# A triangular inverse on VectorE: each final column taken off the columns to its right

## What is computed

```python
lmat = jnp.where(strict, jnp.einsum('bhncd,bhnmd->bhncm', k_beta, k) * decay, 0.0)
tmat = lax.linalg.triangular_solve(eye + lmat, jnp.broadcast_to(eye, lmat.shape),
                                   left_side=True, lower=True, unit_diagonal=True)
u = jnp.einsum('bhncm,bhnmd->bhncd', tmat, v_beta)
w = jnp.einsum('bhncm,bhnmd->bhncd', tmat, k_beta * jnp.exp(gc)[..., None])
```

## Time and profile before

| | us |
|---|---|
| median of 3 runs | 1786.27 |
| lowest and highest | 1786.02, 1787.35 |
| the profiled execution | 1793.27 |
| its span, first to last instruction | 1791.5 |

### The profile page before, as it was taken

How to read it: one execution, slowest core, us unless ns; L and a number is a source line. 1 busy time by engine, 2 the same in 40 slices (tenths; PEclk the granted TensorE clock), 3 DMA queues, 4 the chain that set the end, 5 groups by cost and what they waited for, 6 DMA issues and landing times.

```text
span 1791.5 us, 27755 instructions
## 1 busy us (share of the span) xinstructions
PE 1599.2 (89%) x11576; PEld 1390.4 (78%) x11576; DVE 1022.5 (57%) x1683; ACT 735.2 (41%) x1135; POOL 54.5 (3%) x68
## 2 busy tenths in 40 slices
PE   4998866899989997877899999987999999999987
PEld 2786656888878775655677777766989999999987
DVE  3755799677663655789655554555334343434543
ACT  5555532435345414532224243454543232324454
POOL 0000000000000030000000000000000000000000
PEclk9999978989999988988899999999999999999999
DMA  6254323223232332312221223324323232323222
GB/s 183 79 141 119 88 63 89 75 65 82 61 108 81 80 76 80 96 55 65 66 69 45 60 63 89 99 74 130 100 77 95 83 94 83 95 83 95 87 71 83
DMA packets 281026, 153.37 MB, mean 86 GB/s; under 512 B 36997, under 2 KB 272637, under 8 KB 280894
## 3 DMA queue, kind: packets, MB, share of 16 engines
q1 hardware_dynamic: 279879, 150.32, 29.8%
q10 hardware_dynamic: 1022, 1.28, 0.3%
HBM read 135.03 MB, written 16.97 MB: 85 GB/s over the span
## 4 chain that ended last, share of the span: by engine, by line
PE 68%; DVE 16%; ACT 7%; issue 4%; DMA 4%; ACTq 0%; SPq 0%; POOL 0%; DVEq 0%; POOLq 0%
PE ps L1295 56%; DVE prod L1874 3%; DVE of L1955 3%; PE ps L1429 2%; DVE Xp L1875 2%; DVE w_lo L1628 2%; PE ps L1458 2%; PE ps L1452 1%; DMA w_raw<-in_w_up 1%; DVE tk L1850 1%; ACT L920 1%; PE ps L1278 1%; PE ps L1419 1%; DMA qt<-qkv_dram 1%; ACT w_hi L916 1%
## 5 line engine op out<-in xcount | busy, mean ns | idle before, releaser
L916 ACT ACTIVATE w_hi<-w_raw 128x1024 fp32r<-128x1024 f32 (+3 forms) x258 | 232.7, 902 | 321.1 <-DMA w_raw<-in_w_down 177.9
L1295 PE MATMUL ps<-hh_hi,w_hi 128*128 128x256 f32 (+1 forms) x960 | 323.3, 337 | 30.0 <-DVE w_lo L1628 24.3
L1295 PE MATMUL ps<-hh_lo,w_hi 128*128 128x256 f32 (+1 forms) x960 | 316.7, 330 | 0.0
L1295 PE MATMUL ps<-hh_hi,w_lo 128*128 128x256 f32 (+1 forms) x960 | 315.5, 329 | 0.0
L1628 DVE TENSOR_TENSOR w_lo<-w_raw,w_hi 128x1024 fp32r<-128x1024 f32 (+3 forms) x258 | 266.8, 1034 | 56.5 <-ACT w_hi L916 55.2
L1295 PE MATMUL ps<-u_hi,w_hi 128*128 128x512 f32 (+2 forms) x768 | 260.1, 339 | 24.5 <-DVE w_lo L1628 13.3
L1295 PE MATMUL ps<-u_lo,w_hi 128*128 128x512 f32 (+2 forms) x768 | 253.0, 329 | 0.0
L1295 PE MATMUL ps<-u_hi,w_lo 128*128 128x512 f32 (+2 forms) x768 | 252.0, 328 | 0.0
L1295 PE MATMUL ps<-hm_hi,w_hi 128*128 128x512 f32 (+5 forms) x600 | 212.0, 353 | 28.2 <-DVE w_lo L1628 10.0
L1295 PEld LDWEIGHTS ps<-hh_hi,w_hi 128*128 128x128 f32 x960 | 185.8, 194 | 54.6 <-DVE w_lo L1628 33.9
L1295 PE MATMUL ps<-hm_lo,w_hi 128*128 128x512 f32 (+5 forms) x600 | 201.1, 335 | 0.0
(11 more groups left out here) (274 smaller groups left out, 2169.9 us busy)
## 6 DMA issues: line engine op xcount, KB each, us to landing
w_raw<-in_w_up SPq DMA_DIRECT2D x64, 512.0 KB, 4.1
w_raw<-in_w_in SPq DMA_DIRECT2D x48, 512.0 KB, 4.2
w_raw<-in_w_down SPq DMA_DIRECT2D x64, 256.0 KB, 2.8
w_raw<-in_w_down SPq DMA_DIRECT2D x32, 512.0 KB, 3.7
w_raw<-in_w_out SPq DMA_DIRECT2D x16, 512.0 KB, 3.8
w_raw<-in_w_ple_gate SPq DMA_DIRECT2D x16, 512.0 KB, 3.8
qt<-qkv_dram SPq DMA_DIRECT2D x8, 768.0 KB, 5.5
xin<-in_x_prompt SPq DMA_DIRECT2D x8, 512.0 KB, 6.5
```

Of the source, the lines that this page charges most:

```text
L916: nc.scalar.activation(w_hi[job.slot][:, 0:job.kts, 0:job.m], w_raw[job.slot][:, 0:job.kts, 0:job.m], ACT.Copy).then_inc(w_hid, 1)
L1295: last = nc.tensor.matmul(dst, wt[job.slot][:, k, 0:m], x[:, k, lo:hi], start=(i == 0 and n == 0), stop=(end and n == 2), skip_group_check ...
```

## The change

```diff
--- before.py
+++ after.py
@@ -179,11 +179,11 @@
         h = adv(h)
         put(h, "lp", s)
         put(h, "inv0", s)
-        total, c = sum(x * x + 60 for x in range(1, C)), 1
+        cost = [(x + 1) * (C - 1 - x) + 120 for x in range(C - 1)]
+        c = 0
         for i in range(n):
-            lo, spent = c, sum(x * x + 60 for x in range(1, c))
-            while c < C and (spent < total * (i + 1) / n or i == n - 1):
-                spent += c * c + 60
+            lo = c
+            while c < C - 1 and (sum(cost[:c]) < sum(cost) * (i + 1) / n or i == n - 1):
                 c += 1
             h = adv(h)
             put(h, "inv", s, lo, c)
@@ -1870,10 +1870,11 @@
             def inverse_columns(s, first, end):
                 dve.wait_ge(lt_ld, 16 * (s + 1))
                 for c in range(first, end):
-                    pr = prod[:, 0:c * c].rearrange("p (m j) -> p m j", j=c)
-                    step(nc.vector.tensor_tensor(pr, Xm[:, 0:c, 0:c], bc(Lm[:, 0:c, c], 1, c), ALU.mult))
-                    ins = nc.vector.tensor_reduce(Xm[:, 0:c, c], pr, AX, ALU.add, negate=True)
-                    if c < C - 1:
+                    n = C - 1 - c
+                    pr = prod[:, 0:(c + 1) * n].rearrange("p (m j) -> p m j", j=n)
+                    step(nc.vector.tensor_tensor(pr, bc(Xm[:, 0:c + 1, c], 2, n), bc(Lm[:, c, c + 1:C], 1, c + 1), ALU.mult))
+                    ins = nc.vector.tensor_tensor(Xm[:, 0:c + 1, c + 1:C], Xm[:, 0:c + 1, c + 1:C], pr, ALU.subtract)
+                    if c < C - 2:
                         step(ins)
                     else:
                         ins.then_inc(inv, 1)
```

## The result

The changed kernel takes 1748.33 us, the median of 4 runs (1746.65 to 1750.71), against 1786.14 us for the kernel before in the same session (4 runs, 1785.58 to 1787.35). The ratio is 0.9778 with a 95% interval of 0.9757 to 0.9799: faster, by 37.8 us. The forecast was 1751 us, a saving of 34.9 us, in a range of 1745 to 1760.

What follows compares the result with a forecast made beforehand. DVE was taken to bound both inverse stretches. 1793.27 - 36.4 (DVE) + 1.5 (later engines) = 1758.4 us for the profiled execution; the 34.9 us saving off the median 1786.27 gave 1751 us, range 1745 to 1760.

Steps and rivals of the forecast that it cites:

- The bound: In the stretches of the two inverses, A (69.03 us) and B (69.62 us), DVE has no slack and PE has a lot.
- The old cost: Old column steps: 1.83 ns per product number, 1.05 per sum number, 41.4 us of DVE per inverse.
- The new cost: New column steps: 0.19 us fixed each, 1.04 ns per number, 23.2 us of DVE per inverse.
- rival of the strided column: New product still pays for reading `Xm` with 128 bytes between rows: 8.6 us of gain lost, 1760 us; chance 0.08.
- A price per row: Rival: product and subtraction pay per row jump in `Xm`; break-even 18 ns, at 40 ns 1829 us; slower, chance 0.02.
- What is late next: Check of what becomes late in A and B once DVE needs 50.8 and 51.4 us; 1.5 us allowed in all.
- last `up` jobs of B: Jobs of 24 matmuls where PE or its weights' transfer would be later than DVE by a few tenths of a us.
- PE's wait for ACT in A: One wait of 9.5 us until ACT empties a PSUM bank; claimed to end with a DVE step and move with it.
- rival of PE at the lower clock: PE becomes the bound in A and B: at most 24 us of gain lost, 1759 us (1755 to 1763); chance 0.17.
- wait for the inverses behind B: PE waits 2.21 us for the inverse read back; up to 1.5 us may go, nothing counted.
- The 7 us of the profiled execution: Profiled execution lies 7 us above the runs' median; taken as a difference between executions, so the saving comes off the median.
- more than the DVE time: Rival: PE keeps the upper clock behind either stretch, and the wait behind B shrinks: 3 to 6 us more, 1746 us; chance 0.06.

Runs made afterwards that it cites:

- e1: Kernel before, its old product reading adjacent numbers of a row of Lp instead of a column 128 bytes apart: 1773.76 us, ratio 0.9919.
- e2: Changed kernel, its product reading Lp down a column, 128 bytes apart, instead of along a row: 1761.79 us, ratio 0.9856.
- e5: Changed kernel with only the last of the 31 columns of each inverse computed: 1718.49 us, ratio 0.961.
- e3: Kernel before with the new form for the inverse of half 1 (stretch B) alone: 1771.88 us, ratio 0.9909.
- e4: Kernel before with the new form for the inverse of half 0 (stretch A) alone: 1768.4 us, ratio 0.9887.
- e0: Changed kernel run once more with no edit: 1748.18 us, ratio 0.9784.
- e6: Changed kernel with the columns of half 1 dealt out to 30 stages instead of 12: 1731.57 us, ratio 0.9702; again 1736.2 us, ratio 0.9713.

## Why the prediction came out right

**The bound.** The reading that DVE has no slack in A and B, and that a microsecond less on it is a microsecond less in the end, held. 36.4 us were taken off DVE's queue and the two windows became 138.65 - 102.31 = 36.3 us shorter.

**The old cost** is measured by e1 in the other way: without the stride the product has the price of the sum, 1.16 us for 961 numbers. The 1.83 and 1.05 ns were right.

**The new cost.** 1.04 ns for both steps and 0.19 us fixed gave 0.42 us for the middle column and 23.2 us per inverse; both were measured. L1824 and L1857 were the right neighbours. The rival of the strided column is excluded by the row of 0.42 us, and e2 shows what it would have looked like, 0.62 us and 9 us of time. The prediction gave it 8.6.

**A price per row** is nearly nothing. Products of A in ns: the first column has its 31 numbers in 1 row and the last in 31 rows; the second has its 60 numbers in 2 rows and the last but one in 30:

```profile
L1875 DVE TENSOR_TENSOR prod<-Xp,Lp x1: 186/186/186, 228.3 to 228.3; 128x31 f32<-128x31 f32 x1
L1875 DVE TENSOR_TENSOR prod<-Xp,Lp x1: 209/209/209, 278.9 to 278.9; 128x31 f32<-128x31 f32 x1
...
L1875 DVE TENSOR_TENSOR prod<-Xp,Lp x1: 221/221/221, 228.7 to 228.7; 128x60 f32<-128x60 f32 x1
L1875 DVE TENSOR_TENSOR prod<-Xp,Lp x1: 222/222/222, 278.4 to 278.4; 128x60 f32<-128x60 f32 x1
```

30 more rows cost 23 ns in the last column (20 in its subtraction; 19 and 27 in B), about 0.8 ns each, where 18 ns were needed for no gain. 28 more rows cost 1 ns where a row has two numbers (3 in the subtraction). The start of a row as such is free. The Trainium skill, SBUF — State Buffer, in its note on "cachelines", has every crossing to a new 16-byte line pay the extra cost, and the last column crosses with every number in `Xm`. By this case's price of a crossing, 0.79 ns, 30 of them are 24 ns, and the last column agrees; the last but one, with 28 more crossings for 1 ns, does not. The measurement decides: what is paid for here is a number that stands alone, not every crossing. The old stride of 128 bytes (e1, e2) and L1967's stride of 16 bytes pay the same 0.79 ns. The note's penalty for each crossing leads one to expect that, but its list of what can be strided for free names 4 fp32 numbers, which are these 16 bytes, and there the trace says otherwise.

**What is late next: the term that was too large.** The prediction allowed 1.5 us for PE or ACT becoming the later one at single jobs. The windows are 51.04 and 51.27 us where DVE's time alone gave 50.8 and 51.4: 0.1 us over in sum. The term should have been about nothing. It stood for the last `up` jobs of B, where PE or its weights were to be the later one by a few tenths, and for PE's wait for ACT in A; DVE waited for neither. Nor did the rival of PE at the lower clock come true: its granted clock rose to 0.87 and 0.93, and e5 shows that it goes on rising to 0.95 and 1.00 when DVE's share shrinks further. The wait for the inverses behind B, for which nothing was counted, went from 2.21 us to 1.99:

```profile
810.13 0.34 SPq L750 DMA_DIRECT2D tt_dram<-Xp  x1
816.46 3.13 PE L1419 MATMUL ps<-Vb,Tbd 128*128 128x64 f32 x16 [1.99 <-DMA Tbd<-tt_dram]
```

**The size.** 36.3 us of DVE's time explain most of the 37.8 us of the medians, and the two halves alone (e3 and e4) give 35.8. The forecast of 34.9 is 1.4 us short of that, which is the term above; the 1.5 us that are left have no cause shown and lie inside the interval of the ratio, which reaches from 35.9 to 43.4 us.

**The 7 us of the profiled execution.** The prediction took 1793.27 against a median of 1786.27 for a difference between executions and subtracted from the median. That was needed: the difference of the two spans is 46.2 us, and whoever explains all of it by the change has 10 us too many. The rival "more than the DVE time" would have claimed them, since they lie in part behind A. Against it: the changed kernel's own repeat has 5.5 of them back, and e3, with the old form in A, has 478.8 us in that part. A few microseconds of such a gain could still hide in the spread. The windows of the part between, before, changed, e0 and e6:

```profile
299.60:784.40 484.80, 438.25 (x3560) 370.19 (x3561) 308.92 (x532) 208.93 (x316) 35.14 (x39) 0.92 0.30 80
```

```profile
279.40:755.90 476.50, 430.87 (x3560) 365.76 (x3561) 308.81 (x533) 208.60 (x316) 35.13 (x39) 0.93 0.31 81
```

```profile
279.40:761.40 482.00, 435.25 (x3560) 367.33 (x3561) 308.85 (x533) 209.01 (x316) 35.17 (x39) 0.93 0.30 80
```

```profile
281.50:753.70 472.20, 426.96 (x3560) 362.43 (x3561) 308.67 (x532) 208.66 (x316) 35.17 (x39) 0.94 0.31 82
```

DVE, ACT and POOL are busy for the same time to 0.5 us in all four; PE alone differs, 438.25, 430.87, 435.25 and 426.96 us for the same 3560 matmuls, and its granted clock goes the other way. What makes the clock differ between executions of one kernel is open.

**What to take.** The best version measured is e6, the changed kernel with the second inverse over 30 stages, at 1731.57 and 1736.2 us: 3% below the kernel before and some 12 to 17 us below the changed one.

## To carry to other kernels

Where one engine's queue bounds a stretch without a gap, the sum of durations of what is removed is the forecast, and it holds until the next engine's floor, which a run without the work shows. Ask of each operand whether adjacent numbers of the innermost loop are adjacent in memory: on VectorE an fp32 operand that isn't, and that is not one number repeated either, costs 0.79 ns a number more here, three quarters of the price of a contiguous step. And take a faster step together with its spacing: dealing the columns of B out over more stages gave 13.4 us with the old form and 14.6 with the new one by the traces, on top of what the form gives. When a step is moved, ask also what is placed relative to it: moving taps moved two steps of ScalarE into the scan.

## What was not expected of the hardware

TensorE's granted clock was higher in both kinds of faster stretch, with no change to its work: from 0.85 to 0.93 in B by the new form, and to 1.00 over B in e6 and e5. In B nearly the same matmuls took PE 5.6 us less of busy time. The part between the inverses took from 472.2 to 484.8 us in kernels whose work there is the same, and in the four traces compared all of the difference is in PE, while A and B, bound by DVE, repeat to 0.6 us: a stretch that DVE bounds is the better ruler.
